# A two-layer attention block on one core: scores of a head together, each in two fp32r products, with another order of units and of the first output tiles

## The reference

```python
def diff_attention(q, k, v, lam, chunk_ids):
...
        s = jnp.einsum('bhmqd,bhmkd->bhmqk', qb, k).astype(jnp.float32) * scale
        visible = chunk_ids[None, :] <= cq[:, None]
        s = jnp.where(visible, s, -jnp.inf)
        p = jax.nn.softmax(s, axis=-1)
        a = p[:, :, 0] - lam * p[:, :, 1]
        return jnp.einsum('bhqk,bhkd->bhqd', a.astype(v.dtype), v)
...
def forgetting_attention(q, k, v, cum_logf, positions):
...
        s = jnp.einsum('bhqd,bhkd->bhqk', qb, k).astype(jnp.float32) * scale
        s = s + cq[..., None] - cum_logf[:, :, None, :]
        visible = positions[None, :] <= pq[:, None]
        s = jnp.where(visible, s, -jnp.inf)
        p = jax.nn.softmax(s, axis=-1)
        return jnp.einsum('bhqk,bhkd->bhqd', p.astype(v.dtype), v)
...
    for l in range(DEPTH):
        hn = rmsnorm(h, norm_gain[l])
        proj = hn @ w_in[l]
        ...
        do = diff_attention(dq, dk, dv, lam, chunk_ids)
        do = rmsnorm(do, subln_gain[l], SUBLN_EPS) * (1.0 - lam_init)
        do = jnp.transpose(do, (0, 2, 1, 3)).reshape(b, lp, DIFF_WIDTH)
        do = do * jax.nn.silu(dg)
        ...
        fo = forgetting_attention(fq, fk, fv, cum_logf, positions)
        ...
        h = h + jnp.concatenate([do, fo], axis=-1) @ w_out[l]
```

## Time and profile before

| | us |
|---|---|
| median of 3 runs (1858.14 to 1858.61) | 1858.4 |
| the profiled execution, its own time | 1858.41 |
| its span, first to last instruction | 1856.6 |
| PE busy in the span | 1828.8 |
| DVE, ACT, POOL busy | 1152.6, 770.0, 461.6 |
| attention of layer 0, from its unit 2 | 110.0 |
| attention of layer 1, from its unit 3 | 101.4 |

### The profile page before, as it was taken

How to read it: one execution, slowest core, us unless ns; L and a number is a source line. 1 busy time by engine, 2 the same in 40 slices (tenths; PEclk the granted TensorE clock), 3 DMA queues, 4 the chain that set the end, 5 groups by cost and what they waited for, 6 DMA issues and landing times.

```text
span 1856.6 us, 29611 instructions
## 1 busy us (share of the span) xinstructions
PE 1828.8 (99%) x12020; PEld 1630.2 (88%) x12020; DVE 1152.6 (62%) x1679; ACT 770.0 (41%) x1392; POOL 461.6 (25%) x320
## 2 busy tenths in 40 slices
PE   8999999999999999999999999999999999999999
PEld 8999888979988887999988877989867879999887
DVE  7542465555416657899985555646556589999531
ACT  4122455321235644444433324446565554444331
POOL 5433211354341123000034423320003410000343
PEclk9999999999999999999999999999999999999999
DMA  4222100223220012333323223200003213323223
GB/s 166 94 88 84 42 2 24 74 91 98 82 93 11 24 35 91 115 128 100 103 74 97 96 101 122 83 33 1 1 1 114 91 59 123 126 92 103 72 99 103
DMA packets 41048, 145.49 MB, mean 78 GB/s; under 512 B 5072, under 2 KB 5328, under 8 KB 40784
## 3 DMA queue, kind: packets, MB, share of 16 engines
q1 hardware_dynamic: 40912, 143.59, 23.1%
HBM read 140.40 MB, written 2.10 MB: 77 GB/s over the span
## 4 chain that ended last, share of the span: by engine, by line
PE 90%; DVE 5%; ACT 2%; DMA 1%; issue 1%; POOL 0%; SPq 0%; DVEq 0%; ACTq 0%
PE ps L471 23%; PE ps L472 23%; PE ps L473 23%; PE ps L1069 6%; PE ps L1100 5%; PE ps L1085 2%; PE ps L2673 1%; PE ps L2656 1%; DMA raw<-wstream 1%; DVE xl L563 1%; PE ps L2644 1%; PE ps L1279 1%; PE ps L2414 1%; DVE nm L1146 0%; PE ps L2659 0%
## 5 line engine op out<-in xcount | busy, mean ns | idle before, releaser
L455 POOL TENSOR_TENSOR wl<-raw,wh 128x1024 fp32r<-128x1024 f32 (+1 forms) x168 | 406.9, 2422 | 1024.8 <-ACT wh L447 1024.7
L447 ACT ACTIVATE wh<-raw 128x1024 fp32r<-128x1024 f32 (+1 forms) x178 | 188.9, 1061 | 602.1 <-PE ps L473 536.1
L471 PE MATMUL ps<-xh,wh 128*128 128x264 f32 (+3 forms) x1144 | 384.6, 336 | 4.8 <-ACT wh L447 2.5
L472 PE MATMUL ps<-xl,wh 128*128 128x264 f32 (+3 forms) x1144 | 380.9, 333 | 0.0
L473 PE MATMUL ps<-xh,wl 128*128 128x264 f32 (+3 forms) x1144 | 380.3, 332 | 0.0
L473 PE MATMUL ps<-XSh,wl 128*128 128x256 f32 (+1 forms) x864 | 283.4, 328 | 0.0
L471 PE MATMUL ps<-XSh,wh 128*128 128x256 f32 (+1 forms) x864 | 283.0, 328 | 0.3 <-DVE wl L1752 0.3
L472 PE MATMUL ps<-XSl,wh 128*128 128x256 f32 (+1 forms) x864 | 283.1, 328 | 0.0
L471 PEld LDWEIGHTS ps<-xh,wh 128*128 128x128 f32 x1144 | 215.2, 188 | 31.8 <-issue 9.0
L472 PEld LDWEIGHTS ps<-xl,wh 128*128 128x128 f32 x1144 | 215.3, 188 | 22.7 <-issue 1.2
L473 PEld LDWEIGHTS ps<-xh,wl 128*128 128x128 f32 x1144 | 215.4, 188 | 22.0
(11 more groups left out here) (423 smaller groups left out, 3472.2 us busy)
## 6 DMA issues: line engine op xcount, KB each, us to landing
raw<-wstream SPq DMA_DIRECT2D x176, 512.0 KB, 3.3
rawx<-wpairs SPq DMA_DIRECT2D x44, 512.0 KB, 3.5
raw<-wpairs SPq DMA_DIRECT2D x24, 512.0 KB, 3.5
raw<-wstream SPq DMA_DIRECT2D x10, 528.0 KB, 3.5
h<-xT SPq DMA_DIRECT2D x4, 528.0 KB, 6.1
out<-h SPq DMA_DIRECT2D x8, 256.0 KB, 4.3
xs<-wpairs SPq DMA_DIRECT2D x2, 512.0 KB, 4.4
HF<-wpairs SPq DMA_DIRECT2D x2, 512.0 KB, 5.3
```

What stands on the lines that cost most here:

```text
L447: e.activation(wh[p % 2][:, 0:n], raw[c % 2][:, 0:n], ACT.Copy).then_inc(*w_hi(p))
L455: e.tensor_tensor(wl[p % 2][:, 0:n], raw[c % 2][:, 0:n], wh[p % 2][:, 0:n].bitcast(F32), ALU.subtract).then_inc(*w_lo(p))
L471: e.matmul(o, w_h, x_h, start=start, stop=False)
L472: e.matmul(o, w_h, x_l, start=False, stop=False)
```

## The change

The queries are stored as fp32r: the high part in the 64 rows of its head and the low part in the other 64 (`query_high_act`, `query_low_dve`; for layer 0 the meta queries are also copied to a small zeroed `QZ`). The keys of each head or map are copied by two DMAs per head into both halves of `xs` (`key_copies`), then split by ACT and DVE into a high and a low tensor of 128 rows (`key_high_act`, `key_low_dve`). Their homes are a new `KX`, parts of `wh` and `wl` that rest during attention, and the query slots of heads that are done. A score is then two fp32r products, queries with high keys and queries with low keys. The clearing of `QA` and `QB` is gone.

Units are ordered by head: diff head c with its four query tiles, interleaved with the fox heads 2c and 2c+1, so that units of 144 to 528 keys alternate. `banks_of` lets a unit begin at the first step at which its banks are free (1 to 3 steps ahead). Ends are now those of a head for all four tiles, with one gate instruction where a diff end had four. All transposed tiles of single units are evicted by ACT (every fourth of the diff pairs was by DVE). POOL copies the meta values by quad. Sixteen heads' keys are split per layer, two in the projections and fourteen at the steps of `KEY_STEP`.

In `wout_pe` the first tile is computed whole in columns but without the two last heads' blocks (k = 3 and 7), then three blocks of the second tile, then the two blocks that close the first tile, and the rest of the second. The low part of `wout` tile 2 is made by DVE instead of POOL.

```diff
-V_SPLIT = {(st + part, f) for st in ("ffn1", "ffn2") for part in "gu" for f in range(2, PLAIN)}
+V_SPLIT = {(st + part, f) for st in ("ffn1", "ffn2") for part in "gu" for f in range(2, PLAIN)} | {("wout", l, 2) for l in range(2)}
...
+        def query_high_act(e, on, key):
+            src, to = query_parts(key)
+            on.wait_ge(*(roped[key + ("add", 1)] if key[0] == "dq" else v_out[key]))
+            for j, b in enumerate((0, 64)):
+                r = e.activation(to[b:b + 64, j, :], src[b:b + 64], ACT.Copy)
+            r.then_inc(*a_out(*key, "high"))
+
+        def query_low_dve(e, on, key):
+            kind, l, c = key
+            src, to = query_parts(key)
+            on.wait_ge(*a_out[key + ("high",)])
+            on.wait_ge(*(roped[key + ("add", 1)] if kind == "dq" else v_out[key]))
+            if l == 0:
+                on.wait_ge(*p_one["qz"])
+                for j, b in enumerate((0, 64)):
+                    e.tensor_copy(QZ[b:b + 64, 8 * (kind == "fq") + 2 * c + j, :], src[b:b + 64, 0:16])
+            for j, b in enumerate((0, 64)):
+                r = e.tensor_tensor(to[64 - b:128 - b, j, :], src[b:b + 64], to[b:b + 64, j, :].bitcast(F32), ALU.subtract)
+            r.then_inc(*v_lo(*key))
...
+        KEYS = [("diff", 0, 0), ("diff", 0, 1), ("fox", 0, 0), ("fox", 0, 1), ("diff", 1, 0), ("diff", 1, 1), ("fox", 1, 0),
+                ("diff", 2, 0), ("diff", 2, 1), ("fox", 1, 1), ("fox", 2, 0), ("diff", 3, 0), ("diff", 3, 1), ("fox", 2, 1),
+                ("fox", 3, 0), ("fox", 3, 1)]
+        KEY_STEP = dict(zip(KEYS[2:], (0, 3, 5, 7, 13, 14, 16, 19, 28, 31, 33, 36, 44, 47)))
...
+        def key_copies(e, on, l, kind, c, q):
+
+            i = KEYS.index((kind, c, q))
+            n = 16 * l + i
+            src, made = key_raw(l, kind, c, q)
+            if n >= 4:
+                on.wait_ge(d_key[n % 4], 32 * (n // 4))
+            on.wait_ge(*made)
+            on.wait_ge(*(roped["dk", l, 2 + i, "sin"] if i < 2 else v_lo[("key", l) + KEYS[i - 2]]))
+            for b in (0, 64):
+                e.dma_start(xs[b:b + 64, n % 2, :], src).then_inc(d_key[n % 4], 16)
+
+        def key_high_act(e, on, l, kind, c, q):
+            high, _ = key_home(l, kind, c, q)
+            on.wait_ge(*key_loaded(l, kind, c, q))
+            for s in home_free(l, kind, c, q):
+                on.wait_ge(*s)
+            e.activation(high, xs[:, KEYS.index((kind, c, q)) % 2, :], ACT.Copy).then_inc(*a_out("key", l, kind, c, q))
+
+        def key_low_dve(e, on, l, kind, c, q):
+            high, low = key_home(l, kind, c, q)
+            on.wait_ge(*a_out["key", l, kind, c, q])
+            e.tensor_tensor(low, xs[:, KEYS.index((kind, c, q)) % 2, :], high.bitcast(F32), ALU.subtract).then_inc(
+                *v_lo("key", l, kind, c, q))
...
-            if l:
-                on.wait_ge(*tile["wout", 0, 7])
-                for q, Q in enumerate(Q_of[l]):
-                    e.memset(Q[:, :, :], 0.0).then_inc(*p_one("clear", l, q))
...
+            used, at = {b: -4 for b in range(4)}, [-1]
+            meta = [(12, 21), (28, 35)] if l == 0 else []
+
+            def banks_of(u, wide, to_wide):
+
+                s = max(at[-1], u - 3)
+                while True:
+                    open_ = [b for b in range(4) if used[b] < s]
+                    shut = any(u >= first and s <= last for first, last in meta)
+                    if shut:
+                        open_ = [b for b in open_ if b != META_BANK]
+                    if wide:
+                        fit = [b for b in (0, 2) if b in open_ and b + 1 in open_]
+                    else:
+                        fit = sorted(open_, key=lambda b: (b ^ 1 in open_, used[b]))
+                        if shut and to_wide in (1, 2):
+                            fit = [b for b in fit if (b == META_BANK - 1) == (to_wide == 1)]
+                    if fit:
+                        break
+                    s += 1
+                assert s < u, (u, used, at)
+                at.append(s)
+                for b in range(fit[0], fit[0] + 1 + wide):
+                    used[b] = u
+                return {"banks": (fit[0], 1 + wide), "ahead": u - s}
...
-                    terms.append((Q[:, m, c0:c0 + 128], K[:, m // 2, a:b], a, b, True, not fox and not masked))
+                    terms.append((Q[:, m, c0:c0 + 128], khigh[:, a:b], a, b, True, False))
+                    terms.append((Q[:, m, c0:c0 + 128], klow[:, a:b], a, b, False, not fox and not masked))
...
+            def product(c, ks, first):
+                key = ("wout", l, c)
+                p, o = PART[key], out_of(key, n)
+                on.wait_ge(*w_hi[p])
+                on.wait_ge(*w_lo[p])
+                for i in range(halves):
+                    a = c0 + i * m
+                    for k in ks:
+                        for s in ready(k):
+                            on.wait_ge(*s)
+                        r = mm3(e, o[:, i, :], wh[p % 2][:, 128 * k:128 * k + 128], wl[p % 2][:, 128 * k:128 * k + 128],
+                                X[l][0][:, k, a:a + m], X[l][1][:, k, a:a + m], first and k == ks[0],
+                                not first and k == ks[-1])
+                return r
             next_pair(0)
-            claim(on, pair(key), 2 if n > 512 else 1, v_out[key])
-            for i, part in enumerate(early):
-                part_of_tile(e, on, key, out_of(key, n), *part, layer_ao(l, 2), c0, X[l])
-                if i == 0:
+            for c, ks in ((0, (0, 1, 2, 4, 5, 6)), (1, (0, 1, 2))):
+                claim(on, pair(("wout", l, c)), halves, v_out["wout", l, c])
+                product(c, ks, True)
+                if c == 0:
                     end_pe(e, on, plans[l], *plans[l].held)
-            part_of_tile(e, on, key, out_of(key, n), *late, layer_ao(l), c0, X[l]).then_inc(*tile(*key))
-            for c in range(1, KT):
+            product(0, (3, 7), False).then_inc(*tile("wout", l, 0))
+            product(1, (3, 4, 5, 6, 7), False).then_inc(*tile("wout", l, 1))
+            for c in range(2, KT):
...
-            e.memset(QB[:, :, :], 0.0).then_inc(*p_one("clear", 0, 1))
-            e.memset(QA[:, :, :], 0.0).then_inc(*p_one("clear", 0, 0))
+            e.memset(QZ[:, :, :], 0.0).then_inc(*p_one("qz"))
...
+            for stop, heads in ((CHUNK["va1", l, 0], KEYS[0:2]), (CHUNK["gate", l, 4], KEYS[2:4]),
+                                (CHUNK["wout", l, 2], KEYS[4:])):
+                load_weights(e, on, first, stop)
+                first = max(first, stop)
+                for head in heads:
+                    key_copies(e, on, l, *head)
```

272 lines of the change are left out of this document (170 added, 102 removed).

## The result

The changed kernel takes 1873.4 us (median of 4 runs, 1870.8 to 1875.6), the kernel before 1858.3 in the same session: slower by 0.8%, ratio 1.0080 [1.0068, 1.0093]. The forecast was 1835.2.

The account below looks back on a forecast made before the run. PE, busy 99%, was taken to bound the kernel by its own list. Gains 26.0 + 2.5 + 4.6 = 33.1 us, less 9.9 returned, made 23.2: from 1858.4 to 1835.2 us, range 1822 to 1849.

Parts of the forecast that it names:

- Scores: Attention scores on PE: two fp32r products replace fp32 ones, saving 13.0 us a layer, 26.0 for both (20 to 31).
- Clearings, first `wout` tile and its closing: Outside attention: clearing waits gone, 2.5 us gained; first `wout` tile shorter, 4.6 gained; its closing waits, 1.2 returned.
- What attention gives back: Both attention stages: PE waits for other engines and key copies, 5.2 us a layer, 8.7 after old idling is deducted.
- the sum of units 3 to 9: Early attention steps: DVE has 8.2 us of work against PE's 5.5, so PE waits 2.7 us a layer.
- later the two even out: Later attention: DVE 72.2 us, ACT about 72.3, PE's stage 88.5 in layer 1; 1.5 us a layer more waiting.
- four gates of 0.68 for sixteen of 0.344: Layer 1 attention: fewer gate instructions take 2.0 us off DVE's load, part of its 72.2 us.
- DVE being no denser than 0.72: Rival, chance 0.18: DVE's busy share in attention can't exceed 0.72, so stages are 100.3 and 108.7 us, total 1850.0.
- Late key copies throughout: Rival, chance 0.09: each of 28 key copies in attention exposes a delay on PE; 1869.6 us at 1.3 us each.
- the 1.0 a layer of the sum: Attention: some key copies land up to 0.7 us late before their split, costing PE 1.0 us a layer (0 to 4).
- The ends, priced at part of 1.5 us: Attention: last head's end less covered, priced together with units beginning one step ahead at 1.5 us a layer (0 to 6).

Follow-up runs that it names:

- run 1: Kernel before, in its old order, ends and clearings, with each score as two fp32r products of whole queries and keys, nothing split: 1843.4 us, ratio 0.9922.
- run 2: Changed kernel with one fp32 product of query and high key in place of the two fp32r products: 1889.3 us, ratio 1.0171.
- run 4: Changed kernel without the copies and splits of the fourteen heads' keys in each layer's attention: 1852.2 us, ratio 0.9968.
- run 16: Changed kernel with the fourteen key splits at other steps, mostly away from diff ends, none before step 2: 1860.3 us, ratio 1.0006.
- run 7: Changed kernel with 101 small products against zeros added where PE stood idle: 1869.5 us, ratio 1.0058.
- run 3: Changed kernel with the product with the low keys left out, one fp32r product per score: 1869.0 us, ratio 1.0057.
- run 8: Changed kernel without the DMAs that copy the fourteen heads' keys and ACT's waits for them, splits kept: 1872.5 us, ratio 1.0074.
- runs 6, 10 and 15: Changed kernel with, respectively, ACT's part of diff ends one step later (1876.8 us), `wout`'s second split later (1873.0), ACT's two diff-end functions left out (1877.1).

## Why the prediction was wrong

**Scores: nearly right as PE's work.** 13.0 us a layer were forecast. PE's work fell by 12.3 and 10.1 in the changed kernel, by 13.4 and 12.1 in run 1, and between run 2 and the changed kernel by 13.5 and 12.0. Pairs are a little dearer than I took them (a 400 pair with mask 0.45 and not 0.40, the 272 unit's saving 0.13 and not 0.23).

**Clearings, first `wout` tile and its closing: right in sum.** 2.5 + 4.6 − 1.2 = 5.9 forecast, 5.6 measured. PE starts attention 1.2 us earlier (1.3 forecast), 3.8 lie between the two stages (1.2 + 2.3 − 0.6 = 2.9) and 0.6 behind them (1.7).

**What attention gives back: the step that failed.** The forecast gave 5.2 us a layer, less 1.7: idle time would rise by 8.7. It rose by 25.4. The start of a layer isn't where it failed: 2.7 + 1.0 was forecast there and the first 15 us have 3.2 and 3.3 more idle time than before. In part that is luck, since the sum of units 3 to 9 (DVE 8.2 against PE 5.5) priced each engine's work, and the 2.8 us that came have another reason: DVE's evictions of the last values stand behind a low part whose home comes free only with the projection's last product, a wait that the diff shows. The step that failed is the next one, "later the two even out", with 1.5 a layer (bounds 0 and 6) for units that begin one step ahead and for the ends. Behind the first 15 us idle time rose by 9.5 and 9.4. In run 4, which has the new order and ends and no key work, it rose by 6.6 and 6.7, so most of it comes with order and ends, and no run tells these two apart; 2.9 and 2.7 come with key work. For that part the sum had set DVE's whole load against the stage's length, where what counts is what a low part stands ahead of: run 16, with the same instructions at other steps, gives 13 us back. That each low part delays a maximum for which ACT and then PE's next score wait is my reading of the lists, not shown one by one. DVE's load had a slip too: four gates of 0.68 for sixteen of 0.344 are 2.8 us less, not 2.0, which makes 71.4 for 72.2 and changes nothing here.

**The term that was missing: the clock.** I read 1.00 in every stretch and left it at that. 37.6 us at 1.2 GHz cost up to 18.8, half of the miss of 38.2. In part the gaps bring it: low stretches stand behind six of the seven gaps of over 1.4 us, run 4 loses both together, and run 7, which fills gaps, gets 10.3 slow us back. In part the shorter products do: with nothing else changed, the time at 1.2 GHz is 17.0 us with the fp32 product (run 2), 37.6 with two fp32r products and 61.5 with one (run 3), at idle times of 29.0, 30.6 and 36.7; and run 1 has 17.1 slow us behind gaps hardly longer than those of the kernel before. The longest low stretch of the changed kernel, 10.2 us from 272 us on, has no gap of over 1.1 us in the 20 us ahead of it.

**The rivals.** DVE being no denser than 0.72 came nearest in kind: DVE's share stayed at 0.65 and 0.66 (79.25 of 122.34, 73.39 of 110.90, by the windows after), as before, while I had let it rise to 0.77. Its price of 1850 was too low since 0.72 is an average over a good stretch. Late key copies throughout, my rival for slower, was not it: run 8 gives 1 us, and ACT waited for a copy once in each layer, 1.8 and 1.2 us, near the 1.0 a layer of the sum. The ends, priced at part of 1.5 us, make PE's longest gaps, but runs 6, 10 and 15 show no single wait in them to be the cause; what the old order's cover of them was worth is the 10 us of idle time between runs 4 and 1, of which the ends' share stays open.

## What to carry to other kernels

Where PE is at 99%, freed PE time is worth something only if every other engine's list still runs ahead of it: look in the code's order for what stands ahead of the row that PE waits for, and don't price an added operation on an engine that feeds PE at zero because the engine has idle time: here DVE's low parts cost nearly their full length at the first choice of steps, and all key work 8 us at another. A term for the clock belongs in any sum that takes work from PE: here it ate some 10 of 25 us of saved products with nothing else changed. Before work goes to POOL, see which operations of DVE with both inputs in SBUF fall beside it.
